# Moving the softmax scale of a windowed attention from the output to the probabilities, and deferring the DVE step that takes the output

## The reference

```python
# 8 query heads of 64 channels, 2 key/value heads; blocks of 128 queries
s_loc  = q . k   over the blocks n-1, n, n+1  (|distance| <= 128, else -1e30)
s_ctx  = q . k_context                        (256 context keys)
p = softmax(concat([sink, s_ctx, s_loc]))     # the sink column only enters the sum
o = p_ctx @ v_context + p_loc @ v
mix = o * silu(gate)
```

## Time and profile before

| | |
|---|---|
| median of 3 runs | 3987.47 us (3982.95 to 3995.56) |
| the profiled execution, its own time | 3982.95 us |
| its span | 3979.9 us |
| attention, layer 0: first T to the projection after it | 350.45 to about 493 us |
| attention, layer 1 | 1076.13 to about 1197 us |
| PE busy over the span | 3705.6 us (93%) |
| DVE, POOL, ACT busy | 2075.7, 1411.9, 926.9 us |

### The profile page before, as it was taken

One profiled execution on the slowest core, in us unless ns is written; L12 is line 12 of the kernel. 1 busy time (PEld: TensorE's weight loads), 2 busy tenths in 40 slices (PEclk: granted clock), 3 DMA queues, 4 the chain that ended last, 5 costly groups with the idle time before them and its releaser, 6 DMA issues.

```text
span 3979.9 us, 47179 instructions
## 1 busy us (share of the span) xinstructions
PE 3705.6 (93%) x18764; PEld 2976.4 (75%) x18764; DVE 2075.7 (52%) x2729; ACT 926.9 (23%) x1549; POOL 1411.9 (35%) x918
## 2 busy tenths in 40 slices
PE   5999997899899789998899999999999799999998
PEld 3786786677578667777688888877787578888886
DVE  5675708459581846333464544466323266444556
ACT  3114521321362133222221111113222221111112
POOL 2231013354201345432553333336533363333334
PEclk8999999899899999999999999999999899999999
DMA  5510000231000033110321111114211131111112
GB/s 194 217 32 7 8 22 22 85 130 56 17 2 28 22 131 112 53 32 27 106 77 51 47 42 54 51 38 132 75 32 38 64 106 43 45 53 51 48 40 93
DMA packets 83946, 246.99 MB, mean 62 GB/s; under 512 B 8720, under 2 KB 11792, under 8 KB 82960
## 3 DMA queue, kind: packets, MB, share of 16 engines
q1 hardware_dynamic: 78384, 230.35, 17.7%
q10 hardware_dynamic: 5344, 13.63, 1.0%
HBM read 227.17 MB, written 16.78 MB: 61 GB/s over the span
## 4 chain that ended last, share of the span: by engine, by line
PE 78%; DVE 16%; ACT 2%; issue 2%; DMA 1%; POOL 1%; SPq 0%; DVEq 0%; ACTq 0%; POOLq 0%
PE banks L630 21%; PE banks L628 21%; PE banks L629 21%; DVE wk L1782 2%; PE banks L744 2%; PE banks L758 2%; DVE nt L1687 2%; PE banks L777 2%; DVE h_lo L1703 1%; DVE gw L1917 1%; DVE gw L1906 1%; PE banks L600 1%; DVE nt L1676 1%; PE banks L602 1%; PE banks L601 1%
## 5 line engine op out<-in xcount | busy, mean ns | idle before, releaser
L628 PE MATMUL banks<-h_hi,w_hi 128*128 128x512 f32 (+1 forms) x3504 | 1362.6, 389 | 23.9 <-POOLq L2229 23.9
L630 PE MATMUL banks<-h_hi,w_lo 128*128 128x512 f32 (+1 forms) x3504 | 1348.5, 385 | 0.0
L629 PE MATMUL banks<-h_lo,w_hi 128*128 128x512 f32 (+1 forms) x3504 | 1340.9, 383 | 0.0
L2227 POOL CAST w_hi<-raw 128x1024 fp32r<-128x1024 f32 (+2 forms) x386 | 402.7, 1043 | 2256.4 <-PE banks L630 1865.4
L2228 POOL TENSOR_TENSOR w_lo<-raw,w_hi 128x1024 fp32r<-128x1024 f32 (+2 forms) x386 | 849.7, 2201 | 30.9
L628 PEld LDWEIGHTS banks<-h_hi,w_hi 128*128 128x128 f32 x3504 | 662.3, 189 | 163.7 <-POOLq L2229 29.1
L629 PEld LDWEIGHTS banks<-h_lo,w_hi 128*128 128x128 f32 x3504 | 661.1, 189 | 142.8 <-issue 7.4
L630 PEld LDWEIGHTS banks<-h_hi,w_lo 128*128 128x128 f32 x3504 | 661.6, 189 | 133.1
L2177 DVE TENSOR_SCALAR nt<-wk,v 128x1024 f32<-128x1024 f32 x88 | 87.4, 993 | 391.9 <-ACTq L1619 373.9
L628 PE MATMUL banks<-g_hi,w_hi 128*128 128x512 f32 x704 | 278.8, 396 | 9.3 <-DVEq L2166 6.3
L1424 ACT ACTIVATE wk<-banks 128x512 f32<-128x512 f32 x200 | 118.9, 594 | 680.3 <-PE banks L630 658.0
(11 more groups left out here) (244 smaller groups left out, 4108.0 us busy)
## 6 DMA issues: line engine op xcount, KB each, us to landing
raw<-w_in SPq DMA_DIRECT2D x114, 512.0 KB, 3.6
raw<-w_ffn SPq DMA_DIRECT2D x96, 512.0 KB, 3.5
raw<-w_out SPq DMA_DIRECT2D x64, 512.0 KB, 3.8
raw<-w_down SPq DMA_DIRECT2D x96, 256.0 KB, 2.6
x<-w_mod SPq DMA_DIRECT2D x16, 1024.0 KB, 6.4
wk<-residual SPq DMA_DIRECT2D x48, 256.0 KB, 2.6
gw<-w_mod SPq DMA_DIRECT2D x4, 2048.0 KB, 20.8
residual<-x ACTq DMA_DIRECT2D x4, 2048.0 KB, 10.5
```

What stands on the lines that cost most here:

```text
L628: mm(o, wh[:, ws], hi[:, at_, t0:t0 + n], start=kt == 0, stop=False)
L629: mm(o, wh[:, ws], lo[:, at_, t0:t0 + n], start=False, stop=False)
L630: last = mm(o, wl[:, ws], hi[:, at_, t0:t0 + n], start=False, stop=kt == nk - 1)
L2227: link(G.tensor_copy(w_hi[:, sl], raw[:, sl]))
```

## The change

Each pair's probabilities are divided by their sum before they are transposed, and no longer afterwards on the output. POOL does this in place, with one multiplication by a column for each head, once the reciprocal of the head is there; T(i) now waits for POOL (`p_ready`) instead of for ACT. The two matmuls of line 772 and the second product of X are gone. The output tiles use four places of their PSUM bank in turn (`s % 4`) in place of two. The order on DVE becomes, for each i: X(i-2), C(i), M(i+3), R(i+2). What W waits for is otherwise as before, `mixa_ready` >= s included.

```diff
@@ turn(i), PE
-                    pe.wait_ge(sem["exp_ready"], 2 * s + 2)
+                    pe.wait_ge(sem["p_ready"], s + 1)
@@ weigh(i), PE
                     pe.wait_ge(sem["ptd_copied"], s + 1)
                     if s:
                         pe.wait_ge(sem["mixa_ready"], s)
-                    pe.wait_ge(sem["rec_ready"], 2 * s + 2)
-                    for g in range(2):
-                        c = 8 * (s % 4) + 6 + g
-                        mm(psum[7][g * HD:(g + 1) * HD, (2 + s % 2) * P:(3 + s % 2) * P], at_col[:, c:c + 1].broadcast_to([P, HD]), ident,
-                           start=True, stop=True)
                     for c, kt in enumerate(keys):
                         for g in range(2):
                             hs = slice(g * HD, (g + 1) * HD)
-                            last = mm(psum[7][hs, (s % 2) * P:(s % 2 + 1) * P], at_v[:, kt * P + g * HD:kt * P + (g + 1) * HD],
+                            last = mm(psum[7][hs, (s % 4) * P:(s % 4 + 1) * P], at_v[:, kt * P + g * HD:kt * P + (g + 1) * HD],
@@ mix(i), DVE
-                    link(V.tensor_tensor(m, psum[7][:, (s % 2) * P:(s % 2 + 1) * P], m, ALU.mult))
-                    V.tensor_tensor(m, psum[7][:, (2 + s % 2) * P:(3 + s % 2) * P], m, ALU.mult).then_inc(sem["mixa_ready"], 1)
+                    V.tensor_tensor(m, psum[7][:, (s % 4) * P:(s % 4 + 1) * P], m, ALU.mult).then_inc(sem["mixa_ready"], 1)
@@ the loop of the attention, DVE
                 for i in range(len(pairs)):
+                    if i >= 2:
+                        mix(i - 2)
                     copy_turned(i)
-                    if i:
-                        mix(i - 1)
                     if i + 3 < len(pairs):
                         masked(i + 3)
                     if i + 2 < len(pairs):
                         inverse(i + 2)
-                mix(len(pairs) - 1)
+                for i in range(len(pairs) - 2, len(pairs)):
+                    mix(i)
@@ POOL, after the split of "lr" and the rotary products, ahead of the splits of "cq" and all later ones
+                pairs = PAIRS[l]
+                for i, (j, n) in enumerate(pairs):
+                    s = PAIR0[l] + i
+                    w = len(keys_of(n)) * P
+                    for g in range(2):
+                        c = 8 * (s % 4) + 6 + g
+                        pool.wait_ge(sem["rec_ready"], 2 * s + g + 1)
+                        ps = at_p[s % 3][:, g, 2:2 + w]
+                        last = G.tensor_scalar(ps, ps, at_col[:, c:c + 1], None, ALU.mult)
+                    last.then_inc(sem["p_ready"], 1)
```

More of the change, by code:

```diff
@@ L362, in two_mixers @@
         raw_ready rot_ready cosm_ready rope_ready vt_ready vn_ready vz_ready
-        sc_ready nmax_ready exp_ready rec_ready pt_ready pta_copied ptd_copied o_ready mixa_ready
+        sc_ready nmax_ready exp_ready rec_ready p_ready pt_ready pta_copied ptd_copied o_ready mixa_ready
         z_ready zabs_ready sp_ready la_ready turned v_copied kt_copied cum_ready ex_ready xk_ready kz_split kin_ready
```

## The result

The change is slower: 4078.41 us median of four runs (4068.86 to 4088.94) against 3985.61, a ratio of 1.0227 (95% interval 1.0205 to 1.0248). I had forecast 4046 us and a range up to 4072. The sign and the mechanism of the new wait were right, the size was too small by a third. The profiled execution took 4076.36 us with a span of 4074.6.

The account below looks back on a forecast made before the run. PE was taken to set the pace, DVE close behind, and the order of waits to decide. Attention growth of 32.7 + 30.0 = 62.7 us on 3982.95 gave 4045.7, forecast as 4046 us, range 4030 to 4072.

Parts of the forecast that it names:

- The new wait of W: Attention: W(i-1) waits for X(i-2), now behind M and R; full iterations 5.11 us for 3.97, +62.7 us in all.
- taking out line 772: Attention on PE: value matmuls start 0.27 us earlier per pair, at most 19.4 us over 72 pairs.
- POOL's multiplications: Attention, ahead of T: 0.8 us each taken, two a pair, 1.46 at most; hidden, upper bound 6 us in all.
- My own sign of being wrong: Changed profile: T waiting for POOL in full pairs would show the forecast wrong.
- The argument on the cover: W's wait for X hides POOL: 2.99 us until T is due, plus 1.2 us of lateness, cover even 2.92 us.
- these five iterations: First two and last three of each layer's attention: free of the new loop, minus 4.7 and 5.6 us.
- POOL slower than any row: Rival, attention: over 2 us per POOL operation makes T later than the cover, +0.5 us a pair, 4082 us; chance 0.03.
- Without the cover POOL would be on the path: Attention without the wait for X: POOL's 1.6 us plus handovers exposed, full iterations averaging 3.89 us.
- The clock: Rival: PE's idling lowers its granted clock, 12 us once per couple or 24 twice, 4058 to 4070 us; chance 0.09.
- POOL against DVE: Rival, attention: POOL and DVE hold each other up, M(640) losing 0.72 us, about +43 us, 4089; chance 0.04.
- The other side: Rival, W's wait: X met in time, PE's saving shows, about -15 us, 3968, or -6 with POOL exposed; chance 0.06.
- Four places in PSUM: Output tiles: would allow W ahead of X, but W's wait is unchanged, so worth nothing.

Follow-up runs that it names:

- e12: The changed kernel, unaltered, measured a third time on the control's chip; median below the expected 4072 to 4080 us, outside the attentions 5.7 us shorter than the control.
- e3: The changed kernel with DVE's order of before and POOL multiplying only one column of each head; 3976.86 us, ratio 0.9979, attentions -15.0 us.
- e1: The changed kernel with POOL multiplying only one column of each head, X still deferred; 4054.53 us, ratio 1.0179, attentions +68.5 us.
- e7: The changed kernel with four other forms of POOL's operation: constant factor, copy, product of two tensors, half the columns; single run, 4061.76 us.
- e6: The changed kernel with POOL scaling only three quarters of each head's columns; 4063.35 us, ratio 1.0187, attentions +74.9 us.
- e2: The changed kernel with DVE's order of before, POOL scaling all columns; 4060.13 us, ratio 1.0188, attentions +75.0 us.
- e9: The changed kernel with DVE's order of before and POOL multiplying by the column spread as a second tensor; 4018.02 us, ratio 1.0081, attentions +21.0 us.

## Why the prediction was right or wrong

**What the miss is made of.** The forecast was 4046 us, the first measurement 4078, 32 us more. About 20 of them are in the attentions (82.5 for 62.7), where the largest term is the 14.0 us of POOL's length. The other 12 are outside, where e12 shows no such growth: with the attentions alone the profiled execution would have come to 3982.95 + 82.5 = 4065 us, inside the range of 4030 to 4072. The median of all twelve runs, 4072.1, lies on its edge. So that the first measurement falls clearly outside is in part luck; that POOL's term was wrong is not.

**The new wait of W: right.** Full iterations took 5.17 us for 5.11, W was released by X, beside narrow pairs too, and M began when S ended. The miss of 0.06 is almost all in W, 1.24 for 1.19. In the same way the iteration without either wait is 3.76 us (e3), so that taking out line 772 saved 0.22 us and not the 0.27 between its start and line 777's. Over the 64 waits 0.05 makes about 3 us. X and its handover were 0.41, as taken. With POOL out of the way (e1) the whole came to 68.5 for 62.7; these 3 us and 4.2 of the clock (e1) account for it within 2 us.

**POOL's multiplications: wrong, the step that failed.** I wrote "I take 0.8 each, near the one-input rows, since the second operand is one column", and 1.46 as the upper end; it was 1.88 (e7: 1.81 with a constant). My own sign of being wrong, T waiting for POOL in full pairs, is there (0.90 us at 367.72). The argument on the cover held: at 1.48 POOL costs 6.4 us (e6), within 0.4 of the bound that I gave, and in full iterations even 1.88 fits, since the chain's 9.90 us stand against 2 x 5.17 = 10.34. What is left over falls mostly where no X has to be waited for: on the first iterations of a layer, and the last. I had taken these five iterations to be free of the new loop, and off the sum with 4.7 and 5.6 us. In e1 they were: a couple of layer 1 grew by 9.46 us, four of them would be 37.8, and the attention grew by 31.5. With POOL at 1.88 they were not: 38.1. That, with the falls of the clock that its lateness brings, is the 14.0 us. The rival "POOL slower than any row" (over 2 us, +0.5 us a pair) had the right cause, a price above the measured one, and the wrong place for it, so that its 4082 us, close to the measured 4078, is luck. The Trainium skill ("GPSIMD Engine Reference", section 3.1, Elementwise) speaks against elementwise work on GpSimd, and the 14.0 us agree; by its 2.6 cycles the estimate was 1.4 us, which is nearer than my 0.8 but below the measured 1.88, and above the 1.25 of the form with two tensors.

**Without the cover POOL would be on the path: right, and too small.** I put it at 3.89 us for the average full iteration with a POOL of 1.6 a pair. e2 shows 4.95 with 3.74 a pair, and e9 4.31 with 2.46. Turned round, it stays hidden up to 2 x 3.76 - 6.16 = 1.36 us a pair, a price that none of the forms tried that multiply has at 640 columns.

**The clock: a rival that came in part.** 12 to 24 us were priced for a fall in each couple. It fell once in the change's layer 0 behind the start, for 1.6 us (two iterations of 6.12 and 6.15 where later couples have 5.51 and 5.16), once at the end of layer 1, for another 1.6 us (4.10 for 2.48), and three times in e1, for 4.2 us. Each time PE had stood about 2 us, four times out of five behind a T of 0.66 us; the gaps of 1.3 us in full pairs passed at the upper level, and so did the same 2.00 us in the change's second and third couple. What decides between them the runs don't show. The Trainium skill ("TensorE: Matmul & The Clock Gate", part 1) has the throttled clock as the default that activity lifts; the rows agree.

**POOL against DVE: fell.** M takes 0.82 us with POOL at work beside it (366.86), as in the earlier trace rows. The Trainium skill ("SBUF — State Buffer", section "Who interferes with whom") says that a DVE instruction with at most one input in SBUF, outside its two-port modes, doesn't contend with GpSimd, and the trace agrees.

**The other side: excluded for the right reason.** e3 is that rival made to happen, with -15.0 us in the attentions for the -15 forecast; its median is 6.5 us below before, 3976.86 for the 3968.

**Four places in PSUM: nothing, as forecast.** Whether a looser wait on X would use them was not tried. The places share one bank, and the Trainium skill ("PSUM — Partial Sum Buffer", section "PSUM bank collisions raise a hardware error") says that two engines may not be in one bank at once in the same partitions, even in other columns; no run here shows it.

**Beside the narrow pairs.** There the profile puts W's wait down to ACT's half of C (391.70 in e1), but by the code W(i-1) needs the copy of pair i-1, which is done an iteration earlier; it is X(i-2) that ends last, as the prediction had it. Each such W begins 0.14 to 0.15 us behind the end of X.

**The median.** Three sets of runs put the change 85 to 93 us above before, against 81 to 84 in the attentions; the scatter of unchanged code, 3354 to 3373 us, is wider than what is left. All three leave something over, 1 to 10 us, and where that goes is open.

## What to carry to other kernels

When a step moves in an in-order queue, write down what now stands ahead of it and which semaphore still waits for it: one product of 0.3 us behind 2.12 us of other work cost 68.5 us here, since it closed a loop between PE and DVE. When a profile names what released an instruction, ask the code which event of that name it waits for: the last one to come need not be it. An operation that no row shows gets bounds from both sides that include "slower than the two-input form", and places without cover are costed apart from the steady state. Where two chains run side by side, taking one away shows little (82.5 to 75.0 or 68.5): take both away before a cause is cleared.

## What the runs showed of the hardware

- On POOL a tensor by one column costs 2.5 ns a column (the change: 1883 ns at 640, 923 at 256), by a constant as much (e7: 1809 and 849). That is more than a product of two tensors with the column spread, 1.67 ns (e9: 1254 ns at 640, 615 at 256), and more than twice a copy (e7: 716 ns at 640).
- In e1 the clock fell to its lower level after one gap of 1.99 us (0.68 on average in 390 to 395 us), and the S behind it took 2.50 us in place of 1.35. One late wait beside a narrow pair can so cost 1.5 us more than its own length, and doesn't always: gaps of 2.00 us in the change passed without a fall (1.00 in 405 to 535 us).
- Unchanged code outside the attentions took 3354 to 3373 us from one profiled execution to the next. A single profile can't carry a difference of 10 us there, while the attentions of before repeat to 0.1 us.
